# Ten conv taps ahead of a gate, no product with power zero, ScalarE rounding six weight chunks, FFN weights ahead of stores, U3 gated in another pass, VectorE norming one half

## The reference, cut to what matters

```python
h = rmsnorm(x, norm1_g) * (1 + sc1) + sh1
z = h @ w_in                      # 1024 x 3584: conv (2x512), ssm (512), two gates (2x1024)
y_conv = silu(layernorm(causal_conv31(a * sigmoid(gate)) + conv_b)) @ conv_proj
y = re(C x) + d * u               # x: diagonal complex scan over the 2048 rows, 32 groups x 64 states
za, zb = split(gelu(y) @ ssm_glu);  y_ssm = za * sigmoid(zb)
merged = sigmoid(gl_conv) * y_conv + sigmoid(gl_ssm) * y_ssm
x = x + g1 * (merged @ w_out)
h = rmsnorm(x, norm2_g) * (1 + sc2) + sh2
f_gate, f_up = split(h @ w_ffn_in)           # 1024 x 2*2816
x = x + g2 * ((silu(f_gate) * f_up) @ w_ffn_out)
return rmsnorm(x, final_g)
```

## Time and profile before

| | us |
|---|---|
| three runs | 2541.53, 2543.52, 2545.19 |
| median | 2543.52 |
| profiled execution, its own time | 2545.64 |
| its span (first to last instruction) | 2543.8 |
| TensorE busy | 2490.7 (98%) |
| VectorE busy | 1643.7 (65%) |
| GpSimd busy | 1738.1 (68%) |
| ScalarE busy | 871.4 (34%) |

### The profile page before, as it was taken

How to read it: one execution, slowest core, us unless ns; L and a number is a source line. 1 busy time by engine, 2 the same in 40 slices (tenths; PEclk the granted TensorE clock), 3 DMA queues, 4 the chain that set the end, 5 groups by cost and what they waited for, 6 DMA issues and landing times.

```text
span 2543.8 us, 31372 instructions
## 1 busy us (share of the span) xinstructions
PE 2490.7 (98%) x11419; PEld 2050.3 (81%) x11419; DVE 1643.7 (65%) x2039; ACT 871.4 (34%) x1376; POOL 1738.1 (68%) x1192
## 2 busy tenths in 40 slices
PE   7999999999999999999999999999999999999997
PEld 3888788888888888888788888878888888888886
DVE  5989739945596648946833334485555336889795
ACT  4322411143012421146433345443223334445444
POOL 2776777677866777676887767787777764445555
PEclk9999999999999999999999999999999999999998
DMA  8666347553666347562332232324565337475533
GB/s 279 206 190 216 108 157 224 156 170 115 212 174 190 124 160 222 141 222 86 120 96 75 88 118 77 108 91 141 182 199 175 116 97 245 131 234 178 190 98 108
DMA packets 426161, 395.66 MB, mean 156 GB/s; under 512 B 92232, under 2 KB 330520, under 8 KB 424472
## 3 DMA queue, kind: packets, MB, share of 16 engines
q1 hardware_dynamic: 324688, 319.93, 40.2%
q10 hardware_dynamic: 101320, 73.72, 9.4%
HBM read 317.88 MB, written 67.24 MB: 151 GB/s over the span
## 4 chain that ended last, share of the span: by engine, by line
PE 79%; DVE 12%; DMA 3%; issue 3%; ACT 2%; POOL 1%; ACTq 0%; SPq 0%; DVEq 0%; POOLq 0%
PE bank L1909 18%; PE bank L1911 18%; PE bank L1910 18%; PE bank L2154 4%; PE bank L2156 4%; PE bank L2155 4%; DVE bank L836 3%; PE bank L2070 2%; PE bank L2068 2%; PE bank L2069 2%; DMA row_pair<-in_w_ffn_out 2%; DVE bank L1024 1%; DVE hid_lo L1053 1%; PE bank L1989 1%; PE bank L1974 1%
## 5 line engine op out<-in xcount | busy, mean ns | idle before, releaser
L2238 POOL TENSOR_TENSOR w_lo<-raw,w_hi 128x1024 fp32r<-128x1024 f32 x192 | 480.7, 2504 | 15.4
L2236 POOL CAST w_hi<-raw 128x1024 fp32r<-128x1024 f32 x192 | 209.0, 1089 | 362.4 <-PE bank L1911 277.0
L1909 PE MATMUL bank<-h_hi,w_hi 128*128 128x512 f32 x896 | 352.0, 393 | 0.9 <-ACT wm L1314 0.9
L1911 PE MATMUL bank<-h_hi,w_lo 128*128 128x512 f32 x896 | 349.6, 390 | 0.0
L1910 PE MATMUL bank<-h_lo,w_hi 128*128 128x512 f32 x896 | 349.3, 390 | 0.0
L836 DVE SCALAR_TENSOR_TENSOR bank<-uc,cwt,bank 128x512 f32<-128x512 f32 x464 | 323.1, 748 | 6.2
L2261 POOL TENSOR_TENSOR fw_lo<-fsum,fw_hi 128x512 fp32r<-128x512 f32 x176 | 235.7, 1342 | 74.8 <-ACT fw_hi L1596 74.8
L1909 PE MATMUL bank<-xc_hi_T,fw_hi 128*128 128x512 f32 x704 | 276.0, 392 | 5.6 <-DVE tr L1029 4.2
L1911 PE MATMUL bank<-xc_hi_T,fw_lo 128*128 128x512 f32 x704 | 274.3, 390 | 0.0
L1910 PE MATMUL bank<-xc_lo_T,fw_hi 128*128 128x512 f32 x704 | 274.2, 389 | 0.0
L2293 POOL TENSOR_TENSOR ow_lo<-raw,ow_hi 128x512 fp32r<-128x512 f32 x116 | 160.8, 1387 | 164.2 <-ACT ow_hi L1637 164.0
(11 more groups left out here) (340 smaller groups left out, 5245.8 us busy)
## 6 DMA issues: line engine op xcount, KB each, us to landing
raw<-in_w_in SPq DMA_DIRECT2D x112, 512.0 KB, 3.9
raw<-in_w_ffn_in SPq DMA_DIRECT2D x66, 512.0 KB, 5.8
hid_scratch<-tr SPq DMA_DIRECT2D x88, 256.0 KB, 3.2
raw<-tsum_scratch SPq DMA_DIRECT2D x66, 256.0 KB, 3.2
g2b<-in_w_ada SPq DMA_DIRECT2D x64, 256.0 KB, 3.6
ssm_m<-vk_scratch SPq DMA_DIRECT2D x32, 512.0 KB, 5.1
raw<-in_ssm_glu SPq DMA_DIRECT2D x32, 512.0 KB, 3.6
raw<-in_w_out SPq DMA_DIRECT2D x32, 512.0 KB, 3.7
```

The lines of the kernel that those rows point to most:

```text
L1909: t.matmul(dst, wh, xh, start=first, stop=False)
L1911: return t.matmul(dst, wl, xh, start=False, stop=last)
L2236: g.tensor_copy(hi[:], src[:]).then_inc(hi_done, 1)
L2238: g.tensor_tensor(lo[:], src[:], hi[:].bitcast(F32), ALU.subtract).then_inc(split_done, 1)
```

## The change

Six edits. First, in block 0, 20 taps stand ahead of the last gate and 6 behind it; of `wm` and `vm` the column of power zero is one copy in place of two products and a sum; `mag_k` is made by ScalarE, as first step of `angle_turns`. Second, the last six chunks of w_out in block 3 are rounded by ScalarE (`out_high`), and GpSimd only makes their `w_lo`. Third, ScalarE rounds FFN weights 0 and 1 before the x2 stores and weight 2 between these and the loads of `xr`. Fourth, `gate_u3` gates and adds U3 in steps 2 to 5 of pass 6 (and 13) of a group, out of `combine` of M3. Fifth, GpSimd's and ScalarE's scalings of the half `x3[0]` go; VectorE does them with `final_row`. Sixth, the stores of that half wait for `final_dve`.

```diff
-        CONV = [[tiles_01[:10], tiles_01[10:24], tiles_01[24:] + tiles_23[:-14], tiles_23[-14:]]]
+        CONV = [[tiles_01[:20], tiles_01[20:26], tiles_01[26:] + tiles_23[:-14], tiles_23[-14:]]]
...
+                if j == 0:
+                    link(v.tensor_copy(wm[:, :, s, :], first), "wm")
+                    break
...
+                if j == 0:
+                    link(v.tensor_copy(vm[:, :, 0, :], first))
+                    return
...
-            dve.wait_ge(*scal.after("pro", "m8"))
-            link(v.tensor_copy(mag_k[:, :, 1:], mag_t[:].unsqueeze(2).broadcast_to([P, G, NC])))
...
                 elif name == "M3":
                     step(prod, prod, vs, ALU.add, "C12 sum", "U4")
-                    rows_of("C12", 0, 1, prod, True)
-                    step(ws, ws, g2b[:, 0:HALF], ALU.mult, "U3 gated", "U3")
-                    rows_of("U3", 1, 0, ws, False)
+                    rows_of("C12", 0, 1, prod)
...
+            def gate_u3(g, i):
+                row, ws = x3[1][i][:, 0:HALF], wsum[:, i, :]
+                dve.wait_ge(*outs.after(g, f"C22 sum{i}"))
+                v.tensor_tensor(ws, ws, g2b[:, 0:HALF], ALU.mult).then_inc(*outs.step(g, f"U3 gated{i}"))
+                dve.wait_ge(*outs.after(g, f"U3 gated{i}"))
+                v.tensor_tensor(row, row, ws, ALU.add).then_inc(*outs.step(g, f"U3 rows{i}"))
...
-                if n == 0:
-                    dve.wait_ge(half_rows, TT)
+                dve.wait_ge(final_dve, 6 * (2 * NG - 1))
...
+                if p % 7 == 6 and 2 <= k < 2 + TT:
+                    gate_u3(p // 7, k - 2)
...
             final_over(NG - 1, 0)
+            for i in R(TT):
+                final_row(NG - 1, 0, i)
...
             def angle_turns():
+                act.wait_ge(*scal.after("pro", "m8"))
+                s.activation(mag_k[:, :, 1:], mag_t[:].unsqueeze(2).broadcast_to([P, G, NC]), ACT.Copy)\
+                    .then_inc(*scal.step(0, "mk"))
...
+            def out_high(w):
+                act.wait_ge(raw_in[w % RAW], 16 * ((NB - 1) * (NW // RAW) + w // RAW + 1))
+                act.wait_ge(*chunk_used[NB - 1][w - SPL])
+                s.activation(w_hi[w % SPL][:], raw[w % RAW][:], ACT.Copy).then_inc(out_hi_done, 1)
...
+                        if k in (0, 3, 6):
+                            out_high(NW - 6 + k // 3)
...
-                half_row(i)
-            half_row(TT - 1)
...
-                    g.tensor_copy(hi[:], src[:]).then_inc(hi_done, 1)
-                    pool.wait_ge(hi_done, b * NW + w + 1)
+                    if b < NB - 1 or w < NW - 6:
+                        g.tensor_copy(hi[:], src[:]).then_inc(hi_done, 1)
+                        pool.wait_ge(hi_done, b * NW + w + 1)
+                    else:
+                        pool.wait_ge(out_hi_done, w - NW + 7)
...
-                    g.tensor_tensor(x3[0][i][:], x3[0][i][:], fgb[:], ALU.mult).then_inc(half_scaled_g, 1)
...
-                sp.wait_ge(half_rows, i + 1)
+                sp.wait_ge(final_dve, 6 * (2 * NG - 2) + 3 + i)
```

More of the change, by code:

```diff
@@ L370, in act_steps @@
             if b == 0:
-                names = [f"us{m}" for m in R(KS)] + ["ug0"] + [f"wt{n}" for n in R(8)] + ["kr", "kt", "ug1", "ug2"]
+                names = [f"us{m}" for m in R(KS)] + ["ug0"] + [f"wt{n}" for n in R(8)] + ["mk", "kr", "kt", "ug1", "ug2"]
                 names += [f"kk{n}" for n in R(8)] + ["ka", "sk", "ck", "ug3"] + [f"S{q}" for q in R(NQ)]
@@ L468, in build @@
         raw_in = [sem(f"raw_in{s}") for s in R(RAW)]
-        hi_done = sem("hi_done")
+        hi_done, out_hi_done = sem("hi_done"), sem("out_hi_done")
         split_done = sem("split_done")
@@ L499, in build @@
                                          + i4("U4", "C22 sum", "C22 gated", "C22 rows")
-                                         + i4("C12 sum", "C12 gated", "C12 rows", "U3 gated", "U3 rows")
+                                         + i4("U3 gated", "U3 rows") + i4("C12 sum", "C12 gated", "C12 rows")
                                          + i4("C21 rows")) for g in R(NG)])
@@ L1151, in step, with rows_of @@
                     v.tensor_tensor(dst, x1, x2, op).then_inc(*outs.step(g, f"{name}{i}"))
-                def rows_of(quarter_name, half, f, src, first):
+                def rows_of(quarter_name, half, f, src):
                     cols = slice(f * HALF, (f + 1) * HALF)
-                    if first:
-                        step(src, src, g2b[:, cols], ALU.mult, f"{quarter_name} gated", f"{quarter_name} sum")
+                    step(src, src, g2b[:, cols], ALU.mult, f"{quarter_name} gated", f"{quarter_name} sum")
                     row = x3[half][i][:, cols]
@@ L1565, in mixers @@
                     x_high(0, "T1")
+                    out_high(NW - 3)
                     x_high(0, "T2")
+                    out_high(NW - 2)
                     x_high(0, "T3")
+                    out_high(NW - 1)
+                    w_high(0, 0)
+                    w_high(0, 1)
                 for f in R(1 if last else 2):
@@ L1572, in mixers @@
                             .then_inc(x2_out[i], 16)
+                    if last:
+                        w_high(0, 2)
                     if f == 0:
@@ L1576, in mixers @@
                             act.dma_start(xr[i][:], x_d[bass.ds(b * TB + i * P, P), HALF:]).then_inc(xr_in[i], 16)
-            for b in R(NB - 1):
-                mixers(b, x_d, (b + 1) * TB, 0)
-            for i in R(TT):
-                act.wait_ge(x2_out[i], 1 + 16 * 4)
-            mixers(NB - 1, x2_d, 0, 1, last=True)
             def w_high(q, i):
@@ L1596, in w_high @@
                 s.activation(fw_hi[i][:], src, ACT.Copy).then_inc(whi_done, 1)
+            for b in R(NB - 1):
+                mixers(b, x_d, (b + 1) * TB, 0)
+            for i in R(TT):
+                act.wait_ge(x2_out[i], 1 + 16 * 4)
+            mixers(NB - 1, x2_d, 0, 1, last=True)
             def copy_product(q):
@@ L1637, in weight_high @@
                 s.activation(ow_hi[n % OW][:], fraw[n % 4][:, 0:HALF], ACT.Copy).then_inc(ow_hi_done, 1)
-            w_high(0, 0)
-            for i in R(1, 5):
-                w_high(0, i)
+            w_high(0, 3)
+            w_high(0, 4)
             x_high(0, "B22")
```

17 lines of the change are left out of this document (4 added, 13 removed).

## The result

The changed kernel took 2531.30 us (median of 4 runs, 2529.16 to 2532.69) against 2544.36 for the kernel before beside it: ratio 0.9948, 95% interval 0.9936 to 0.9961. Taken once more, it gave 2530.56 against 2545.98, ratio 0.9939 (0.9924 to 0.9954). So the change saves 13 to 15 us; 2522.6 us had been forecast, with 2530 as the upper end, and a saving of 20.9. The spans of the profiled executions are 2543.8 and 2527.4, 16.4 apart; where these 16.4 come from is read first.

A forecast was written before the change was run, and what follows sets the result against it. TensorE, busy 98% of the span, was taken as the bound, so only its waits could go. Terms 5.5 + 3.1 + 0.6 + 11.7 = 20.9 us took 2545.64 to 2524.7, less 2.12 gave 2522.6; range 2518 to 2530.

The forecast's parts named there:

- block 0: Term for block 0: TensorE's ys_lo wait, its slow-clock stretch and a dt wait go; 5.5 us, bounds 3 to 6.2.
- the switch: Switch to the FFN: w_lo waits go (2.8 us), GpSimd's earlier start gives 0.3; 3.1 us, bounds 1 to 5.
- the end: Last steps: last matmul starts at 2524.3 instead of 2535.97; 11.7 us, bounds 9 and 12.3.
- the zero for the powers: Block 0: the four operations of the zero powers cost or give nothing where VectorE waits for ScalarE; zero.
- the second way: Switch gives nothing: GpSimd runs into VectorE's two-input operations, later loads delay residual rows; 3.1 us off, 2525.7; chance 0.13.
- U3: Gating U3 four steps earlier in pass 6 removes a 0.78 us wait before 2360.66; 0.6 us, bounds 0 and 0.9.
- the last row sum: ScalarE, last steps: 6.8 us of work ahead of it goes, so it starts at 2510 instead of 2515.41.
- the price of the final rows: Four rows on VectorE, 1.4 to 2.5 us each beside the last 36 matmuls; TensorE waits 0.4 us, 1.3 at most.
- the fourth way: Last steps: final rows and three ow_lo hold one another up, clock falls to 0.50; 5 us lost, 2527.6; chance 0.15.
- The last step of the sum: From profiled execution to median of runs: 2.12 us taken off, 2524.7 to 2522.6.
- two ways partly together: High end of the range, 2530: holds block 0's gain failing (2528.1), the end giving part (2527.6), and two partly together.
- The slower side: ScalarE's FFN weights ahead of stores and residual loads stall on fsum; a 30 us wait gives 2548; chance 0.04.

The follow-up runs named there:

- taps back: Changed kernel with 10 and 14 taps around the last gate as before; 10.1 us under the kernel before by medians, ratio 0.9956.
- block 0 alone: Kernel before with only the block 0 edits (taps, power zero copies, mag_k on ScalarE); 5.3 us under the kernel before by medians, ratio 0.9979.
- switch alone: Kernel before with only `out_high` and the moved `w_high` (ScalarE's output chunks and FFN weights); 2.9 us under the kernel before by medians, ratio 0.9991.
- U3 back: Changed kernel with U3 gated in combine of M3 again, final rows still on VectorE; 13.6 us under the kernel before by medians, ratio 0.9944.
- Rows late: Changed kernel with VectorE's four final rows waiting for the last ow_lo; 15.7 us under the kernel before by medians, ratio 0.9938.
- together: Changed kernel plus early Silu table load, steps 151 and 152 rounded before last row sum, U3 two steps earlier, final rows behind last ow_lo; 2526.02 us against 2545.93.
- half back: Changed kernel with the last group's first half scaled by GpSimd and ScalarE again; 11.2 us under the kernel before by medians, ratio 0.9957.
- rounding first: Changed kernel with ScalarE rounding chunks of steps 151 and 152 ahead of the last row sum; 18.2 us under the kernel before, ratio 0.9927.

## Why the prediction was wrong
Laid out by stages, the first profile of the changed kernel misses 4.5 of the 20.9 us: block 0 gave 0.5 more, the stretch from the switch to step 150 with pass 8 in it 0.4 more, the switch 1.8 less, the end 3.5 less (8.2 for 11.7), the tail 0.1 less.

**Block 0, right.** 5.5 forecast, 5.95 and 5.59 in the two profiles of the changed kernel, 5.3 alone. The steps were those written: ten taps into the idle time, ys_lo held by ScalarE's tr, the slow clock gone. That the ten taps are the cause is shown by taps back, and so is the zero for the powers.

**The switch, mechanism half right, size wrong.** The two waits on w_lo went, and 5.2 us were won by matmul 5859, more than the 3.1 counted. The step that failed is the sentence that of GpSimd's earlier start only 0.3 us could be found. It left out what the earlier TensorE then meets. That was written down as the second way, GpSimd running into VectorE's two-input operations, but there as a loss at the place of the w_lo, not as a new wait one column step later that gives back 2.3 us and takes the clock down for 1.6 more. Net 1.3.

**U3, right.** 0.6 was forecast, with 0.9 as the upper bound; 0.94 came. The wait of the earlier trace rows is in pass 8, two passes behind the one in which U3 is gated, but it hangs on VectorE's backlog from there. In the four kernels that gate U3 in combine of M3 (before, block 0 alone, switch alone, U3 back) VectorE's last final row of pass 8 ends at 2351.5 to 2351.6 on the times of before, and TensorE waits 0.8 to 1.1 us; in the ten others it ends at 2349.2 to 2349.7, and there is no wait. U3 back differs from the changed kernel in U3's place alone. The prediction's words, a stretch where VectorE and ScalarE run late, are what the traces show; that the backlog lasts for two passes it did not say.

**The end, the failed step.** The term was 11.7 us; it gave 8.2, and 6.7 in the second profile. Two steps of its working failed. First, the last row sum. The forecast took the operations of U3 out from ahead of it, 6.8 us, and let the combining begin when it began before; so it had the row sum 5.4 us sooner, at 2510. U3's operations don't vanish, they stand ahead of the combining in the same queue, which begins 5.5 us later for them, and the row sum comes 2.6 us sooner, at 2512.8: 3.5 us ahead of the time at which TensorE wants step 151 (2507.33 + 0.23 - 2504.04), not 6.0. U3 back shows that U3's place doesn't move it at all once the scalings are off GpSimd. Second, and the larger part, the price of the final rows. They were put beside the 36 matmuls, and the three ow_lo beside them were given 0.4 us of waiting, 1.3 at most. The waits were 0.79 + 1.40 + 1.40 = 3.6 us (from start to start, less 0.23 for a matmul). Rows late shows the share of the contention: with the row sum as late as in the changed kernel, and the rows out of the way, the end gives 10.9. With the rounding ahead of the row sum as well, in together, it gives 12.1. What came is the fourth way, in the first profile without its clock, in the second with it: 3.5 and 5.0 us less than forecast, where 5 had been written.

The page GPSIMD Engine Reference of the Trainium skill (section 8, Key points) names VectorE instructions with two SBUF inputs as those that contend with GpSimd. The trace agrees: 1.98 against 1.22 us a row, 2.2 against 1.27 us an ow_lo. The forecast cited it and then priced it as one rival with 0.15, when the trace of before already had both operations at several lengths: six final rows at 1.27 and two at 2.31 us, ow_lo from 1.25 to 2.33.

**The last step of the sum, too.** 2.12 us were taken off because the median of before lay that far under its profiled execution. That was one draw of the scatter (2542.5 to 2547.5 us for the kernel before in one series) and no property of the kernels: the profiled execution of the changed kernel was the fastest of its four runs, 2.14 under their median. So of the 8.7 us by which the median missed, 4.5 are in the profiles and 4.3 are this. The range allowed for two ways partly together, which is what came, but not for this step as well.

**The slower side** didn't come near: fsum began 9.7 us sooner than before, and TensorE has no wait for a residual row.

## What to carry to other kernels
When several stages ahead of a wait get faster, take the time at which the waiting engine comes from the sum of them, and the time at which its releaser is ready from the releaser's own chain; the difference of two shifts is what is won or lost, and the wait may simply move to the next place at which the slower of them is needed. Work moved earlier in an engine's queue still delays all that is queued behind it, here two passes on; work moved behind the last thing that somebody waits for frees that wait, but may be given back in the tail (2.8 us here). An operation moved between VectorE and GpSimd should be priced at its contended length as well as at its own, and so should what stands beside it.

## What the runs showed of the hardware
The same wait of TensorE was followed by a granted clock of 0.50 in some profiles and not in others, in two places. Behind the wait of about 2.6 us on tr it fell in the changed kernel both times, and with U3 back, half back and rounding first; with switch alone, rows late and taps back the wait was as long and the clock stayed at 1.00 there (matmuls 5907 to 5930 keep their lead), while at about 1673 to 1682 us those three kernels, and together, have a stretch at 0.50 that the others don't have. That one costs nothing in the end: 1.6 us are lost and come back by matmul 7783, as the next wait, on xc_lo_B, is 0.8 us instead of 2.4. Behind the three waits for ow_lo in the last steps it fell in four profiles of six. What decides between them is not settled here; in either place it moves a result by about 1.6 us, as much as many of the differences that are at issue in such work.
